# Two blocks on one core: two-sided filters built from summed and differenced taps, and high and low rows in one 512-column operand

## The reference

```python
# filters for positions 0..L-1, two directions, two orders, 1024 channels
h = jnp.sin(fr * (z @ w1 + b1)); ...; h = (h @ w4).reshape(L, 2, 2, 1024)
h = h * decay
k = concatenate([h_fwd, zeros, h_bwd[:0:-1]], axis=0)
k_f = rfft(k / sum(abs(k), axis=0), axis=0)

def long_conv(z, k_f, bias):
    y = irfft(rfft(z, n=2 * L, axis=1) * k_f, n=2 * L, axis=1)[:, :L]
    return y + z * bias
# p: short convolution of three taps per channel, split in v, x1, x2
z = x1 * long_conv(v, k_f[:, 0], bias[0])
z = x2 * long_conv(z, k_f[:, 1], bias[1])

u, v = split(gelu(p_sgu)); y_sgu = u * spatial(layernorm(v))
merged = sigmoid(g_hy) * (y_hy @ w_branch_hyena) + sigmoid(g_sgu) * (y_sgu @ w_branch_sgu)
x = x + merged @ w_out; x = x + ffn(rmsnorm(x))
```

## Time and profile before

| what | value |
|---|---|
| time, median of 3 runs (lowest, highest) | 2855.32 us (2849.82, 2855.89) |
| span of the profiled execution | 2846.2 us |
| time outside that span, median less span | 9.1 us |
| TensorE busy | 2699.9 us, 95% |
| TensorE weight loads busy | 2261.9 us, 79% |
| VectorE busy | 1867.1 us, 66% |
| ScalarE busy | 1276.0 us, 45% |
| DMA | 651.39 MB, mean 229 GB/s |

### The profile page before, as it was taken

One profiled execution on the slowest core, in us unless ns is written; L12 is line 12 of the kernel. 1 busy time (PEld: TensorE's weight loads), 2 busy tenths in 40 slices (PEclk: granted clock), 3 DMA queues, 4 the chain that ended last, 5 costly groups with the idle time before them and its releaser, 6 DMA issues.

```text
span 2846.2 us, 36151 instructions
## 1 busy us (share of the span) xinstructions
PE 2699.9 (95%) x14454; PEld 2261.9 (79%) x14454; DVE 1867.1 (66%) x2410; ACT 1276.0 (45%) x1567; POOL 28.9 (1%) x50
## 2 busy tenths in 40 slices
PE   3879999998999999999899899999999999999998
PEld 1468898776888888887698599999778888888886
DVE  6997765876577889898876445545565454445445
ACT  2134544443444577777533144443444434443443
POOL 1000000000000000000000000000000000000000
PEclk9789998998999999999999999999999999999999
DMA  9898784523777899999444254554556556555553
GB/s 358 324 366 299 284 316 147 209 101 115 256 265 266 285 363 371 374 370 369 176 177 180 86 213 163 178 177 163 193 177 192 192 188 195 185 189 193 190 192 118
DMA packets 181648, 651.39 MB, mean 229 GB/s; under 512 B 12395, under 2 KB 12460, under 8 KB 137464
## 3 DMA queue, kind: packets, MB, share of 16 engines
q1 hardware_dynamic: 170496, 593.53, 58.9%
q0 software_dynamic: 8160, 37.17, 3.5%
q10 hardware_dynamic: 2840, 18.56, 1.7%
HBM read 641.82 MB, written 13.68 MB: 230 GB/s over the span
## 4 chain that ended last, share of the span: by engine, by line
PE 76%; DVE 10%; DMA 7%; ACT 3%; issue 3%; DVEq 0%; SPq 0%; ACTq 0%
PE ps L1769 74%; DMA raw<-in_stream 7%; DVE raw L1102 2%; DVE w_lo L1023 2%; ACT w_hi L626 2%; PE ps L1921 1%; DVE arena L1084 0%; DVE arena L1198 0%; DVE arena L1648 0%; PE ps L1888 0%; DVE arena L1646 0%; DVE arena L1647 0%; PE ps L2330 0%; DMA under_r<-in_c_row 0%; DVE h_lo L1074 0%
## 5 line engine op out<-in xcount | busy, mean ns | idle before, releaser
L1023 DVE TENSOR_TENSOR w_lo<-raw,w_hi 128x1024 fp32r<-128x1024 f32 x968 | 1171.4, 1223 | 784.0 <-ACT w_hi L626 780.0
L626 ACT ACTIVATE w_hi<-raw 128x1024 fp32r<-128x1024 f32 x968 | 1011.1, 1057 | 1022.3 <-PE ps L1769 931.4
L1769 PE MATMUL ps<-w_hi,h_hi 128*128 128x512 f32 x1216 | 476.9, 392 | 12.0 <-DVE w_lo L1023 10.2
L1769 PE MATMUL ps<-w_hi,r_hi 128*128 128x512 f32 x1184 | 468.9, 396 | 9.9 <-DVE w_lo L1023 3.0
L1769 PE MATMUL ps<-w_lo,h_hi 128*128 128x512 f32 x1216 | 474.8, 390 | 0.0
L1769 PE MATMUL ps<-w_hi,h_lo 128*128 128x512 f32 x1216 | 474.8, 390 | 0.0
L1769 PE MATMUL ps<-w_hi,r_lo 128*128 128x512 f32 x1184 | 462.5, 391 | 0.0
L1769 PE MATMUL ps<-w_lo,r_hi 128*128 128x512 f32 x1184 | 462.3, 390 | 0.0
L1769 PE MATMUL ps<-h_hi,w_hi 128*128 128x256 f32 x1536 | 441.0, 287 | 8.1 <-DVE w_lo L1023 3.6
L1769 PE MATMUL ps<-h_lo,w_hi 128*128 128x256 f32 x1536 | 436.2, 284 | 0.0
L1769 PE MATMUL ps<-h_hi,w_lo 128*128 128x256 f32 x1536 | 436.0, 284 | 0.0
(11 more groups left out here) (303 smaller groups left out, 1899.8 us busy)
## 6 DMA issues: line engine op xcount, KB each, us to landing
raw<-in_stream SPq DMA_DIRECT2D x524, 1024.0 KB, 5.7
under_r<-in_stream SPq DMA_DIRECT2D x47, 512.0 KB, 6.9
arena<-in_mod_units ACTq DMA_DIRECT2D x16, 1024.0 KB, 5.6
arena<-in_stream SPq DMA_DIRECT2D x20, 512.0 KB, 6.3
under_h<-in_stream SPq DMA_DIRECT2D x13, 512.0 KB, 5.0
bias_skew<-bias_rows POOLq DMA_DIRECT2D x4, 1536.0 KB, 16.4
filters<-arena POOLq DMA_DIRECT2D x4, 1280.0 KB, 5.6
arena<-filters POOLq DMA_DIRECT2D x4, 1280.0 KB, 6.2
```

What stands on the lines that cost most here:

```text
L626: act.activation(dst, src, ACT.Copy).then_inc(hi_ready, 1)
L1023: dve.tensor_tensor(low, src, high, ALU.subtract).then_inc(lo_ready, 1)
L1769: return pe.matmul(o, a, b, start=start, stop=stop)
```

## The change

It has two parts.

**Filters.** The features of the positions are now kept in 128 rows: rows 0 to 63 hold them once, rows 64 to 127 hold them again with position 0 zeroed, once with the same sign (`F_SUM`) and once negated (`F_DIFF`). The weights `w4` are stacked the same way, forward columns in the upper 64 rows and backward in the lower. One product then gives the sum (or difference) of forward and backward taps, so VectorE's four additions go; the DFT products read `taps` directly. For the norm, |a| + |b| is taken as the larger of |a+b| and |a-b|: ScalarE takes the absolute values in two passes, VectorE two maxima (`taps_largest`), and the norm products are eight. 1/norm is no more applied to the spectra: it goes into the short convolution's weights and bias of the first 16 tiles (v and x1, `conv_cols`), once. The Hyena bias times norm is accumulated on TensorE by three products of 512 columns with `ones` against diagonals (`bias_diag`). ScalarE copies the five spectra out of PSUM. The load that spread `hyena_bias` over all partitions (1 MB) is replaced by one of 16 x 128.

**Rows.** `h_hi`, `h_lo` and `r_hi`, `r_lo` become halves of `h_two`, `r_two`, at the same addresses. In hyena, sgu_u, gate_hy, gate_sgu and branch_hy a chunk is now one product of the high weights with both halves (2 x 256 columns, the two results side by side in a bank) and one of the low weights with the high half. VectorE adds the two results (`add_halves`) to SBUF and reports on one semaphore, `halves_added`; convolution, gelu, sigmoid and product read from there, gelu and sigmoid one step later. TensorE waits on `halves_added` for its banks, also across the ends of gate_hy and branch_hy. branch_sgu keeps `three`.

```diff
-        h_hi = sb("h_hi", [P, DC, T], F32R)
-        h_lo = sb("h_lo", [P, DC, T], F32R)
+        h_two = sb("h_two", [P, 2, DC, T], F32R)
+        h_hi, h_lo = h_two[:, 0, :, :], h_two[:, 1, :, :]
...
             load("ld_bias", (at(F_RELB, 32, parts=32), d["rel_bias"]), (arena[32:36, F_RELB:F_RELB + 32], d["owner"]),
-                 (at(F_ONEH, 384, parts=36), d["onehot"]))
+                 (at(F_ONEH, 384, parts=36), d["onehot"]),
+                 (at(F_HYB, P, parts=16), d["hyena_bias"].rearrange("b (q n) -> (b q) n", q=4)))
...
-            load("ld_block", (w4, d["filt_w4"].rearrange("b p n -> p b n")),
-                 (decay.rearrange("p b t n -> p b (t n)"), d["decay"][0:2].rearrange("b p n -> p b n")),
-                 (hyena_b.rearrange("p b n -> p (b n)"), d["hyena_bias"].rearrange("b n -> (b n)").partition_broadcast(P)))
+            load("ld_block", (w4[0:64], d["filt_w4"][:, :, 0:512].rearrange("b p n -> p b n")),
+                 (w4[64:128], d["filt_w4"][:, :, 512:1024].rearrange("b p n -> p b n")),
+                 (decay.rearrange("p b t n -> p b (t n)"), d["decay"][0:2].rearrange("b p n -> p b n")))
...
+            for name, sign in ((F_SUM, 1.0), (F_DIFF, -1.0)):
+                act.activation(at(name, T, parts=64), at(F_H, T, parts=64), ACT.Copy).then_inc(sem("taps_rows"), 1)
+                act.activation(arena[64:128, name:name + 1], at(F_H, 1, parts=64), ACT.Copy, scale=0.0).then_inc(sem("taps_rows"), 1)
+                act.activation(arena[64:128, name + 1:name + T], arena[0:64, F_H + 1:F_H + T], ACT.Copy, scale=sign)\
+                    .then_inc(sem("taps_rows"), 1)
...
+            abs_taps(0)
             for b in range(4):
...
                 for q in range(4):
-                    ins = act.activation(rn_diag[:, q, :], ident, ACT.Copy, scale=rn_cols[:, q:q + 1])
-                ins.then_inc(sem("rn_act"), 1)
+                    ins = act.activation(bias_diag[:, q, :], ident, ACT.Copy, scale=bias_cols[:, q:q + 1])
+                ins.then_inc(sem("bias_ready"), 1)
+                if b < 3:
+                    abs_taps(b + 1)
...
-                copy(rnorm[b % 2], ps[:, 2, :]).then_inc(sem("rn_act"), 1)
+                for place, n in enumerate((2, 3, 0, 1, 4)):
+                    act.wait_ge(sem("spectrum_mm"), 5 * b + place + 1)
+                    copy(ko[b % 2][:, n, :], ps[:, 3 + n, :]).then_inc(sem("spectrum_out"), 1)
...
             def sigmoid(dst, name):
+                def tile(n):
+                    act.wait_ge(sem("halves_added"), 4 + SPLIT[name] + n + 1)
+                    act.activation(dst[:, n, :], dst[:, n, :], ACT.Sigmoid).then_inc(sem("gates_out"), 1)
...
             for b in range(4):
-                dve.wait_ge(sem("norm_mm"), b + 1)
...
-                for t in range(TH):
-                    for op, o in ((ALU.add, 0), (ALU.subtract, 2)):
-                        dve.tensor_tensor(taps_abs[b % 2][:, o + t, :], taps[b % 2][:, 2 * t, :], taps[b % 2][:, 2 * t + 1, :], op)\
-                            .then_inc(sem("parity_ready"), 1)
                 if b < 3:
                     make_taps(b + 1, 0, 2)
+                dve.wait_ge(sem("norm_mm"), b + 1)
+                ch(dve.reciprocal(rn_all[:, 4 * b:4 * b + 4], ps[:, 2, 0:4]))
+                dve.tensor_tensor(bias_cols, ps[:, 2, 0:4], col("hyb", 16)[:, 4 * b:4 * b + 4], ALU.mult).then_inc(sem("rn_ready"), 1)
                 modulation(done_units, 1)
                 if b < 3:
                     make_taps(b + 1, 2, 4)
-                modulation(done_units + 1, 6)
+                modulation(done_units + 1, 2)
+                if b < 3:
+                    taps_largest(b + 1)
+                modulation(done_units + 3, 4)
                 done_units += 7
...
-                for n in range(5):
-                    dve.wait_ge(sem("spectrum_mm"), 5 * b + n + 1)
-                    dve.tensor_tensor(ko[b % 2][:, n, :], ps[:, 3 + n, :], rnorm[b % 2], ALU.mult)\
-                        .then_inc(sem("spectrum_out" if n in (2, 3) else "spectrum_cos"), 1)
-                dve.wait_ge(sem("spectrum_cos"), 3 * b + 3)
-                for n in (0, 1, 4):
-                    o = ko[b % 2][:, n, :]
-                    dve.tensor_tensor(o, o, hyena_b[:, b, :], ALU.add).then_inc(sem("spectrum_out"), 1)
...
+            def add_halves(dst, bank):
+
+                dve.tensor_reduce(dst, ps[:, bank, :].rearrange("p (u n) -> p n u", u=2), AX, ALU.add).then_inc(sem("halves_added"), 1)
...
+            def feature_split(k, o):
+
+                half = k % 2 * 8
+                for j in range(8):
+                    c, a = half + j, w(k, j * P, P)
+                    mm(o.rearrange("p (u n) -> p u n", u=2), a[0], h_two[:, :, c, :], c == 0, False)
+                    ins = mm(o[:, 0:T], a[1], h_hi[:, c, :], False, c == DC - 1)
+                return ins
...
+            def spectrum(b):
+
+                pe.wait_ge(sem("taps_ready"), 4 * b + 4)
+                parts = ((cosm, 0, 0), (cosm, P, 0), (sinm, 0, 2), (sinm, P, 2), (nyq, 0, 0))
+                for place, n in enumerate((2, 3, 0, 1, 4)):
...
+                pe.wait_ge(sem("bias_ready"), b + 1)
+                for n in (0, 1, 4):
+                    mm(ps[:, 3 + n, :].rearrange("p (q n) -> p q n", q=4), ones[:, :], bias_diag, False, True).then_inc(sem("spectrum_mm"), 1)
...
-            pe.wait_ge(sem("spectrum_cos"), 10)
+            pe.wait_ge(sem("spectrum_out"), 18)
             turn("h1", xh=x)
...
             def gate_step(g, i, k):
...
                 if k % 2 == 0:
-                    pe.wait_ge(sem("sg1_out"), 4 * i + (k // 2 + 1))
-                return feature_major(k, ps[:, k // 2, 0:T])
+                    pe.wait_ge(sem("halves_added"), SPLIT["gate_hy"] + 4 * i + (k // 2 + 1))
+                return feature_split(k, ps[:, k // 2, :])
             phase("gate_hy", gate_step, unrolled=True)
-            pe.wait_ge(sem("sg1_out"), 4 + 16)
-            branch("branch_hy", 0, "bhy_out")
+            branch("branch_hy", 0, "halves_added", SPLIT["branch_hy"])
```

More of the change, by code:

```diff
@@ L128, in moe_unit @@
     return (p, u) if u < 8 else (p - 1, u)
+SPLIT = {"hyena": 0, "sgu_u": 24, "gate_hy": 32, "branch_hy": 48, "gate_sgu": 64}
 BASE, UNITS = {}, 0
@@ L931, in _, with gelu_tile @@
             seq_out(11)
+            def gelu_tile(n):
+                act.wait_ge(sem("halves_added"), 4 + SPLIT["sgu_u"] + n + 1)
+                act.activation(uT[:, n, :], uT[:, n, :], ACT.Gelu).then_inc(sem("gates_out"), 1)
             def gelu_u(g, i, k):
-                if k % 2:
-                    done(g, k)
-                    act.activation(uT[:, bass.ds(4 * i + k // 2, 1), :],
-                                   ps[:, k // 2:k // 2 + 1, 0:T], ACT.Gelu)\
-                        .then_inc(sem("u_out"), 1)
+                n = 8 * i + k - 2
+                if n >= 0 and n % 2:
+                    gelu_tile(n // 2)
             def u_step(g, i, k):
@@ L947, in gelu_v @@
             def gelu_v(g, i, k):
+                if i == 0 and k == 1:
+                    gelu_tile(7)
                 if k % 8 == 7:
@@ L955, in sigmoid @@
             def sigmoid(dst, name):
+                def tile(n):
+                    act.wait_ge(sem("halves_added"), 4 + SPLIT[name] + n + 1)
+                    act.activation(dst[:, n, :], dst[:, n, :], ACT.Sigmoid).then_inc(sem("gates_out"), 1)
                 def step(g, i, k):
-                    if k % 2:
-                        done(g, k)
-                        act.activation(dst[:, bass.ds(4 * i + k // 2, 1), :], ps[:, k // 2:k // 2 + 1, 0:T], ACT.Sigmoid)\
-                            .then_inc(sem(name), 1)
-                return step
-            first_gate = sigmoid(sg1, "sg1_out")
+                    n = 8 * i + k - 2
+                    if n >= 0 and n % 2:
+                        tile(n // 2)
+                return step, tile
+            first_gate, first_tile = sigmoid(sg1, "gate_hy")
+            second_gate, second_tile = sigmoid(sg2, "gate_sgu")
             def gate_step(g, i, k):
@@ L974, in _ @@
             phase("gate_hy", gate_step, unrolled=True)
+            first_tile(DC - 1)
             phase("branch_hy")
-            phase("gate_sgu", sigmoid(sg2, "sg2_out"))
+            phase("gate_sgu", second_gate, unrolled=True)
+            second_tile(DC - 1)
             def merged_hi(g, i, k):
@@ L1701, in _, with second_gate @@
             phase("gate_hy", gate_step, unrolled=True)
-            dve.wait_ge(sem("sg1_out"), 4 + 16)
+            dve.wait_ge(sem("gates_out"), 8 + 16)
             def branch_step(g, i, k):
                 done(g, k)
-                t = sg1[:, bass.ds(8 * i + k, 1), :]
-                dve.tensor_tensor(t, t, ps[:, k % 4:k % 4 + 1, 0:T], ALU.mult).then_inc(sem("bhy_out"), 1)
-            phase("branch_hy", branch_step)
-            phase("gate_sgu")
-            dve.wait_ge(sem("sg2_out"), 4 + 16)
-            dve.wait_ge(sem("bhy_out"), 4 + 16)
```

(17 more changed lines are left out.)

141 lines of the change are left out of this document (79 added, 62 removed).

## The result

The changed kernel takes 2834.1 us (median of 4 runs, 2831.1 to 2837.4) against 2854.5 for the kernel before (4 runs beside it, 2849.8 to 2855.9): a ratio of 0.9929, interval 0.9912 to 0.9945, a gain of 20.4 us. It is faster, as forecast; the size is 14 us short of the forecast 34.5.

A forecast was written before the change was run, and what follows sets the result against it. TensorE, busy 95% of the span with 76% of the chain, was taken as the bound. 15.0 (products) + 0.5 (ends) + 19.0 (filters) = 34.5 us; span 2846.2 becomes 2811.7, plus 9.1 gives 2821 us, range 2808 to 2836.

The forecast's parts named there:

- rival 2: Half-units: the fixed cost stays although there are fewer products, so a half-unit saves nothing; time 2836 us; chance 0.07.
- The half-unit of 8 x (226.8 + 119.9) ns: Hyena, sgu_u, gates, branch_hy: eight wide and eight narrow products take 2774 ns, in place of 24 x 119.9 = 2878 ns.
- rival 3: Wide products: reading two pieces 16 KB apart holds TensorE up; kernel slower from 257 ns a product; chance 0.05.
- The term of 15.0 us: Hyena, sgu_u, gates, branch_hy: fewer products save 104 ns a half-unit, times 144 half-units.
- then 15.9 for seven sums and 1.0 of waiting: End of filter stage: from the 34th sum over units to the first instruction after the filters, 16.9 us against 21.0.
- rival 1: Filter stage: TensorE becomes the bound at low clock, saving 9 us in place of 19; time 2831 us; chance 0.12.
- the bytes alone ... which from 50.7 on is 143: Filter stage: its bytes need 92 us at 413 GB/s, ending at 143 us, so DMA does not forbid the saving.
- stores of the filters start as copies end, no later than now: Filter stage: filter stores begin when ScalarE's copies end, no later than before; no cost was put on it.
- 19.0: Filter stage: saving in us, with the first instruction after the filters at 150.8 against 169.8 us.
- The term of 2.6 us for the removed load: Start of filter stage: dropping the 1 MB `hyena_bias` broadcast takes 2.6 us off, at 402 GB/s.
- 0.5 (ends): Phase ends in the rows' part: shorter waits give 1.5 us, later sums cost 0.3 and 0.7, leaving 0.5 us.
- Rival 4: Rows' part: a VectorE sum of halves takes 1.3 us or more, so some 15 us go; chance 0.04.

The follow-up runs named there:

- experiment 4: Changed kernel with the eight wide products of a half-unit ahead of its eight narrow ones, not in turn: 2834.8 us, ratio 0.9945 to the kernel before.
- experiment 5: Changed kernel with each wide product cut into two of 256 columns, sums of halves kept: 2844.6 us, against 2830.6 for the changed kernel on the same occasion.
- Rows alone: Kernel before with only the rows' part (two-half operand, sums of halves), filters as before: 2848.2 us, ratio 0.9969 to the kernel before.
- the late store: Changed kernel with the last filter store and the bias-row spreading behind it held until VectorE has consumed all units: 2829.8 us, and 2828.8 on another occasion.
- experiment 3: Changed kernel with the 1 MB load of `hyena_bias` put back, read by nothing but waited for: 2832.2 us, ratio 0.9939 to the kernel before.
- filters alone: Kernel before with only the filters' part, still 24 products of 256 columns: 2845.7 us, ratio 0.9965 to the kernel before.
- experiment 1: The changed kernel again (2834.4 us), and the kernel before with only the rows' part (2848.2 us) or only the filters' part (2845.7 us).

## Why the prediction was right, and where it was short

**Direction, place and mechanism were right.** Faster, by two parts that both work alone, at 2834 in a range of 2808 to 2836, but close to its end. That the range reached so far is in part luck: its end was put by rival 2, and what made the gain small were other things.

**The wide product was right in rate.** The half-unit of 8 x (226.8 + 119.9) ns stands in the chain as 11.10 us for four of them. Two pieces 16 KB apart cost nothing over a contiguous operand at the quick pace and 3 ns in experiment 4, and were all of the slow pace theirs, 6.6, where rival 3 needed 30; and experiment 5 gives back 13.9 us in the time, 9 to 15 in the profiles, for the products of the old width (rival 2, that the cost per product would stay). Here the trace and the Trainium skill, "TensorE: Matmul & The Clock Gate", section "Wait — 56ns, not 53.3ns?", part: its 2.5 ns a product would make experiment 5 an estimated 2.9 us slower, and it was 13.9 (9 to 15 in the profiles).

**The term of 15.0 us was too large all the same, by the second pace.** It was worked out for one pace in all 144 half-units: 226.8 + 119.9 ns. Sampled windows of after give 353.3 ns a pair through all 80 half-units of the gates and branch_hy, 348.2 on average in hyena and 347.9 in sgu_u. Over the forecast that is 80 x 8 x 6.6 ns = 4.2 us, and 48 x 8 x 1.5 + 16 x 8 x 1.2 ns = 0.7 us: 15.0 becomes 10.1. No row of the kernel before has a product of 512 columns in turn with one of 256, and I took the sum of two rows, each of products of one width, as certain.

**The clock was left out of that part.** The forecast took hyena's 0.99 for the whole group. After has falls at 1543.8, 1557.5 and 1748.6 us, 3.4 us each, that the kernel before has not: 5.1 us. So the second block comes to 10.1 + 0.5 - 5.1 = 5.5 us, and its stretch is 6.3 us shorter in the profile after. Rows alone come to 10.1 + 0.5 - 3.4 (a fall of 6.8 us in its profile) = 7.2, less 1.9 as all of its hyena runs at 353 ns: 5.3, where its stretch is 6.4 shorter and the time 8.9.

**The filter stage failed in the last leg: "then 15.9 for seven sums and 1.0 of waiting".** The blocks went as forecast or better: VectorE did not wait 2.3 us a block for TensorE after the 13th sum, and TensorE's clock was mostly full (rival 1 was wrong). I had checked DMA only by "the bytes alone ... which from 50.7 on is 143", and this went wrong three times. The rate was 338 GB/s until 90 us, as SyncE waited there for VectorE to free the buffers (30.6 of 36.7 us): 36.7 x (1 - 338/413) = 6.7 us. It was 395 in the late store's profile and not 413 after that: 2.7 us. With these the floor is 152.4, which is where the late store has the mark (152.8, 152.6); this agrees partly by construction, as the rates are those of the stage that ends there. And "stores of the filters start as copies end, no later than now" I put down as harmless: earlier was the harm, some 3.8 us, with 2.9 MB put ahead of the last units. 19.0 becomes 13.4.

**The term of 2.6 us for the removed load was right in its place and worth nothing at the end**, since a stage that DMA bounds later absorbs all but some tenths of a microsecond of it (experiment 3).

**The account.** 13.4 (filters) + 10.1 (products) + 0.5 (ends) - 5.1 (clock) = 18.9 us against 20.4 measured. Rival 4 was wrong: 0.69 us a sum, all hidden, no wait for `w_lo` in the changed phases. Two of the forecast's numbers beside the sum were wrong as well: rivals 4 and 1 together take 15 + 10 us of 34.5, which leaves 9.5 us of gain and not less than 5; and 188 GB/s in hyena becomes 195 by a half-unit of 2774 in place of 2878 ns, not 192 (192 were measured, at the slower mean pace). Neither changes the forecast.

**What stays open.** Why the falls of the clock at `spatial` come with the rows' part: experiment 5 has one at the old widths, rate and count of products, so the wide products are not needed for it, and no run told apart what is left. Two profiles without a fall are few, too. Nor is it settled what picks one of the two paces; a pace holds through long runs of half-units (in two profiles the gates change from 353.3 to 346.6 at `spatial`, in the others not). Why the mark is 3.3 us earlier in the two kernels with `spatial` spread is open. In filters alone the mark gains 12.9 us and the time 10.0, which the interval covers. The table of experiment 1 puts the difference between the mark and hyena, where all twelve profiles with the new filters have 1237.5 to 1244.7 us and the two with the old ones 1233.1 and 1235.1. But those two were of executions 6 to 9 us quicker than their kernels' medians, so whether the new filters give something back there or these two were quick by chance is not settled.

## What to carry to other kernels

When an engine is relieved in a stage, add up the bytes of that stage in their order: a store that becomes ready earlier goes ahead of loads that are late, and to hold it back was worth 3.8 us of the stage here. When a product is made wider, the saving is the cost per product times the products that go, but look at the pace of the new mix in the trace before counting it in every phase, and look where the clock now falls: here it fell at a stretch of short products, and in the two profiles where they were spread among long ones it did not, though the time showed no sure gain. A gain early in a stage is worth nothing if its end is set by something else.

## What the runs showed of the hardware

- Products of 512 and 256 columns in turn, each with its weights, run at one of two paces, 346.7 or 353.3 ns a pair, and stay at it for 64 products (pieces in hyena, 11.10 and 11.30 us) to over a thousand (the gates). Eight of 512 and then eight of 256 have one pace, 349.4 ns.
- A product of high weights with two pieces of 256 columns, 16 KB apart, costs about as much as a contiguous one of 512 columns: 346.9 ns a pair at the quick pace against 226.8 + 119.9, and 230 ns against 226.8 in groups of eight.
- Four fp32 products of 128 columns (eight instructions) go from 1.16 to 2.08 us as the granted clock falls from 2.4 to 1.2 GHz, while TensorE shows as busy throughout: a busy share of 100% does not say that the clock is full.
- One core's DMA held 393 to 406 GB/s from 90 to 150 us in the twelve profiles with the new filters, where loads of units, stores of filters and the spreading of the bias rows shared it, and 402 to 415 in short windows before.
